# Sums of squares of a grouped norm: transposes and running sums in place of products with ones

## The reference

```python
N_GROUPS = 8
D_INNER = 2 * D_MODEL            # 2048, 256 channels a group
def ssd_branch(z, xbc, dt_raw, ...):
    xbc = silu(causal_depthwise_conv(xbc, conv_w, conv_b))
    ...
    y = ssd_chunked(...)                     # chunked scan of the 32 heads
    y = y * jax.nn.silu(z)
    yg = y.reshape(bsz, seqlen, N_GROUPS, D_INNER // N_GROUPS)
    yg = yg * lax.rsqrt(jnp.mean(yg * yg, axis=-1, keepdims=True) + RMS_EPS)
    y = (yg.reshape(bsz, seqlen, D_INNER) * norm_g)
    return y @ out_w
```

## Time and profile before

| | |
|---|---|
| time, median of 3 runs | 923.46 us (922.59 to 923.56) |
| profiled execution, first to last instruction | 922.0 us |
| TensorE matmuls busy | 910.9 us, 99% |
| VectorE busy | 752.3 us, 82% |
| ScalarE busy | 551.0 us, 60% |
| GpSimd busy | 18.3 us, 2% |
| granted TensorE clock, mean of the core | 0.999 |

### The profile page before, as it was taken

How to read it: one execution, slowest core, us unless ns; L and a number is a source line. 1 busy time by engine, 2 the same in 40 slices (tenths; PEclk the granted TensorE clock), 3 DMA queues, 4 the chain that set the end, 5 groups by cost and what they waited for, 6 DMA issues and landing times.

```text
span 922.0 us, 18238 instructions
## 1 busy us (share of the span) xinstructions
PE 910.9 (99%) x6625; PEld 860.2 (93%) x6625; DVE 752.3 (82%) x1373; ACT 551.0 (60%) x938; POOL 18.3 (2%) x30
## 2 busy tenths in 40 slices
PE   8999999999999999999999999999999999999997
PEld 6999989999999999998888888999999999999886
DVE  5999999999999888689888646798859988888543
ACT  5649666776667474556666535668455765666432
POOL 1000000000000000000000000100000000000000
PEclk9999999999999999999999999999999999999999
DMA  8576234545445537437555554455147455555601
GB/s 326 180 265 227 93 127 170 205 130 188 148 148 205 206 105 276 169 128 246 198 182 183 195 190 166 144 176 189 61 166 266 156 191 182 182 182 182 228 1 47
DMA packets 45470, 161.55 MB, mean 175 GB/s; under 512 B 5188, under 2 KB 5864, under 8 KB 45288
## 3 DMA queue, kind: packets, MB, share of 16 engines
q1 hardware_dynamic: 43488, 154.74, 48.6%
q10 hardware_dynamic: 1928, 6.08, 1.8%
HBM read 159.72 MB, written 1.09 MB: 174 GB/s over the span
## 4 chain that ended last, share of the span: by engine, by line
PE 62%; issue 24%; DVE 10%; ACT 1%; DMA 1%; POOL 0%; SPq 0%; DVEq 0%; POOLq 0%; ACTq 0%
PE A L436 8%; PE A L437 8%; PE A L438 8%; PE B L656 5%; PE A L465 4%; DVE w_lo L1330 3%; PE B L465 3%; PE B L436 2%; PE B L437 2%; PE B L438 2%; PE A L467 2%; DVE part L1366 2%; PE B L467 2%; PE B L737 2%; PE B L816 1%
## 5 line engine op out<-in xcount | busy, mean ns | idle before, releaser
L1330 DVE TENSOR_TENSOR w_lo<-raw,w_hi 128x1024 fp32r<-128x1024 f32 x265 | 321.5, 1220 | 67.7 <-ACT w_hi L888 66.2
L888 ACT ACTIVATE w_hi<-raw 128x1024 fp32r<-128x1024 f32 x265 | 276.4, 1052 | 79.6 <-PE A L738 20.9
L436 PE MATMUL A<-h,w_hi 128*128 128x256 f32 x952 | 274.1, 288 | 0.0
L438 PE MATMUL A<-h,w_lo 128*128 128x256 f32 x952 | 269.3, 283 | 0.0
L437 PE MATMUL A<-h,w_hi 128*128 128x256 f32 x952 | 269.3, 283 | 0.0
L436 PEld LDWEIGHTS A<-h,w_hi 128*128 128x128 f32 x952 | 182.2, 191 | 1.9 <-issue 1.8
L437 PEld LDWEIGHTS A<-h,w_hi 128*128 128x128 f32 x952 | 182.4, 192 | 0.2
L438 PEld LDWEIGHTS A<-h,w_lo 128*128 128x128 f32 x952 | 182.2, 191 | 0.0
L436 PE MATMUL B<-h,w_hi 128*128 128x256 f32 x352 | 100.9, 287 | 0.0
L437 PE MATMUL B<-h,w_hi 128*128 128x256 f32 x352 | 99.6, 283 | 0.0
L438 PE MATMUL B<-h,w_lo 128*128 128x256 f32 x352 | 99.6, 283 | 0.0
(11 more groups left out here) (301 smaller groups left out, 1560.8 us busy)
## 6 DMA issues: line engine op xcount, KB each, us to landing
raw<-in_weights_dram SPq DMA_DIRECT2D x289, 512.0 KB, 4.1
csrow<-cs_dram ACTq DMA_DIRECT2D x9, 512.0 KB, 4.5
x<-in_x_dram SPq DMA_DIRECT2D x4, 256.0 KB, 5.1
bd<-in_lru_w_dram ACTq DMA_DIRECT2D x1, 1024.0 KB, 6.8
out_dram<-m_wide SPq DMA_DIRECT2D x3, 256.0 KB, 2.1
raw<-in_weights_dram SPq DMA_DIRECT2D x2, 256.0 KB, 4.9
par<-in_params_dram SPq DMA_DIRECT2D x1, 379.0 KB, 7.1
out_dram<-m_wide ACTq DMA_DIRECT2D x2, 128.0 KB, 2.5
```

What stands on the lines that cost most here:

```text
L436: mm(dst, wh, lo, start=first, stop=False, skip_group_check=free)
L438: return mm(dst, wl, hi, start=False, stop=last, skip_group_check=free)
L888: F(w_hi[:, s, :], raw[:, s, :], ACT.Copy).then_inc(hi_ready, 1)
L1330: V.tensor_tensor(w_lo[:, s, :], raw[:, s, :], w_hi[:, s, :].bitcast(F32), ALU.subtract).then_inc(lo_ready, 1)
```

## The change

TensorE no longer multiplies squares with ones. As soon as the gated `y` is there it transposes `y`, four blocks of 128x128 into bank `A[3]`, so that tokens lie on the partitions and a group's 256 channels on the free axis. ScalarE squares each half (128 x 256) straight from PSUM and keeps a running sum over the free axis (`accum_out`) in a new tile `ysum` of 128 x 2. VectorE reads the moment from `ysum`.

In turns 1 to 7 the transposes stand in the middle of the second output piece. In turn 0, which has no output piece, they stand where the products with ones stood. On ScalarE the squares move: behind `first_taps` in the loop, and in the first turn from n = 6 to n = 8.

```diff
@@ in TensorE's program
-            def y_sums(g):
-                pe.wait_ge(ysq_ready, g + 1)
+            def y_transposes(g):
+                pe.wait_ge(yz_ready, g + 1)
                 for t in range(TT):
                     for c in range(2):
-                        ins = mm(sums[:, t:t + 1], ysq[:, c, t * P:(t + 1) * P], ones[:, 0:1],
-                                 start=c == 0, stop=c == 1)
-                ins.then_inc(sums_ready, 1)
+                        ins = nc.tensor.transpose(A[3][:, t * T + c * P:t * T + (c + 1) * P], y[:, c, t * P:(t + 1) * P],
+                                                  ident)
+                ins.then_inc(yt_ready, 1)
...
-            def out_piece(p, turn, g, c):
+            def out_piece(p, turn, g, c, between=None):
                 native_loaded(p, turn)
                 pe.wait_ge(scale_read, g + 2)
                 for m in range(KD):
+                    if between is not None and m == KD // 2:
+                        y_transposes(between)
                     ins = mm(acc_out(m), raw[:, p % RING, m * P:(m + 1) * P], yn[:, c, :], start=False, stop=False,
...
-            chain = {1: cb, 2: x_transposes, 3: y_products, 4: y_sums, 5: y_scale}
+            chain = {1: cb, 2: x_transposes, 3: y_products, 5: y_scale}
...
-                        out_piece(base + OUT_AT[s // 4], t, g - 1, s // 4)
+                        out_piece(base + OUT_AT[s // 4], t, g - 1, s // 4, g if s == 4 else None)
...
-            first_chain = {1: cb, 3: x_transposes, 5: y_products, 7: y_sums, 8: y_scale}
+            first_chain = {1: cb, 3: x_transposes, 5: y_products, 7: y_transposes, 8: y_scale}
@@ in ScalarE's program
             def y_squares(g):
-                act.wait_ge(yz_ready, g + 1)
-                F(ysq[:, :, :], y[:, :, :], ACT.Square).then_inc(ysq_ready, 1)
+                act.wait_ge(yt_ready, g + 1)
+                for t in range(TT):
+                    ins = F(ysq[:, t, :], A[3][:, t * T:(t + 1) * T], ACT.Square, accum_out=ysum[:, t:t + 1])
+                ins.then_inc(sums_ready, 1)
...
                 split(6)
+                act.wait_ge(cb_used, g + 1)
+                first_taps(g + 1, (0, 1))
+                act.wait_ge(yz_ready, g + 1)
+                first_taps(g + 1, (2, 3))
                 y_squares(g)
-                first_taps(g + 1)
                 drain_input(4, 4, base + IN_AT[4], t)
...
                     if n == 6:
+                        act.wait_ge(yz_ready, 1)
+                        first_taps(1)
+                    if n == 8:
                         y_squares(0)
-                        first_taps(1)
@@ in VectorE's program
             def y_mean(g):
-                moment_of(g + 2, 2 * P, RMS_EPS).then_inc(mean_ready, 1)
+                moment_of(g + 2, 2 * P, RMS_EPS, ysum[:, :]).then_inc(mean_ready, 1)
```

More of the change, by code:

```diff
@@ L223, in hybrid_kernel @@
         dt_parts = ysq[:, 0, :]
+        ysum = sb("ysum", [P, TT], scope=s3)
         s3.close()
@@ L331, in hybrid_kernel @@
         dec_ready, m_ready, y_ready, yz_ready = sem("dec_ready"), sem("m_ready"), sem("y_ready"), sem("yz_ready")
-        ysq_ready, first_tap = sem("ysq_ready"), sem("first_tap")
+        yt_ready, first_tap = sem("yt_ready"), sem("first_tap")
         conv_operand_ready, mixed_ready = sem("conv_operand_ready"), sem("mixed_ready")
@@ L681, in _ @@
                 if s in (1, 4):
-                    out_piece(GATES0 + OUT_AT[s // 4], 0, g - 1, s // 4)
+                    out_piece(GATES0 + OUT_AT[s // 4], 0, g - 1, s // 4, g if s == 4 else None)
                 if s in chain:
@@ L956, in ring, with first_taps @@
                 return A[o % 3][:, 0:T]
-            def first_taps(g):
+            def first_taps(g, js=range(4)):
                 act.wait_ge(drained, drained_by(g, 3))
                 dyn = not isinstance(g, int)
-                for j in range(4):
+                for j in js:
                     at = (g * 4 + j) * SSM_K + SSM_K - 1
```

## The result

The changed kernel takes 927.20 us (median of 5 runs, 925.48 to 927.62) against 923.20 us for the kernel before (5 runs, 922.59 to 923.56): ratio 1.0041, 95% interval 1.0030 to 1.0052. It is slower by 0.3 to 0.5%. 926.3 us had been forecast. The profiled execution has a span of 925.7 us against 922.0.

The account below looks back on a forecast made before the run. TensorE bounds turns 2 to 6, VectorE leads in turn 0, early turn 1 and late turn 7. Span 922.0 - 2.4 (loop) + 4.3 (stall) + 0.95 (clock) = 924.85, plus 1.46 gives 926.3 us; range 925.2 to 927.6, 80% 923.9 to 928.6.

Parts of the forecast that it names:

- The stall in turn 0: VectorE's moment waits 5.0 us for ScalarE's squares behind the exponents; 0.72 us absorbed, 4.3 us more.
- The clock: TensorE, idle 6.4 us in turn 0, restarts at 1.2 GHz; loses 1.6 us, 0.65 hidden, 0.95 us more.
- chance (a): Rival: turn 0's stall comes but TensorE's clock holds; 925.4 us, chance 0.20.
- The loop's gain: TensorE in turns 1 to 6: products with ones save 0.89 us, transposes cost 0.49; net 0.40 a turn, 2.4 us less.
- about 0.57 us of room: Loop: GpSimd's scale is ready at 166.12, TensorE takes it at 166.74; only gain above 0.57 us would be lost.
- one of the prediction's own signs of being wrong: Loop: the forecast is wrong if the scale starts to hold TensorE there.
- Where each turn's gain ends: Turns 1 to 6 pay 0.40 us each; in turns 0 and 7 the gain goes into TensorE's wait for the scale.
- That room on VectorE: VectorE's waits for TensorE in the loop, 0.98 us a turn, shrink to 0.58.
- The price of a transpose: TensorE: four cost 0.43 to 0.53 us, taken as 0.49; the page's 275 ns is a latency, not a cost.
- The sum: Whole kernel: 922.0 - 2.4 + 4.3 + 0.95 = 924.85 us for the span, 926.3 us for the median.
- The step from span to median: Whole kernel: the median stands 1.46 us above the profiled span, so 924.85 becomes 926.3 us.
- its three bounds: Whole kernel: stall 4.0 to 4.8 us, gain 1.8 to 3.3, clock 0 to 2.2.

Follow-up runs that it names:

- The run with early squares: Changed kernel with turn 0's squares on ScalarE moved ahead of the twelve exponents (n = 6 instead of n = 8): 921.95 us, ratio to the kernel before 0.9985.
- the one with the stall alone: Kernel before with turn 0's squares moved to n = 8 behind first taps, products with ones just ahead of the scale, no transposes: 930.71 us, ratio 1.0076.
- the run with fillers: Changed kernel plus 24 filler matmuls of 512 columns on TensorE while it stands idle in turn 0: 926.23 us, ratio to the kernel before 1.0033.
- the early moment: Changed kernel with turn 0's squares ahead of the exponents and, in turns 1 to 7, VectorE's moment ahead of the split: 920.29 us, ratio 0.9969.
- the fastest version: The same kernel as the early moment: squares of turn 0 ahead of the exponents, moment ahead of the split in turns 1 to 7: 920.29 us.

## Why the prediction was right

**The stall in turn 0** was the main term and came as forecast: ScalarE's squares at 111.14 (111.63 said, and the whole stage was 0.5 us earlier), VectorE's wait 4.95 us (5.0 said), the scale at 113.18 (113.7). Two squares with their sums took 0.72 us (0.8 said). The wait of 0.72 us for `w_hi` went. The run with early squares took the stall out and the one with the stall alone put it into the kernel before; both support the mechanism.

**The clock** fell, as forecast, with TensorE idle for 6.28 us (6.4 said), but this step's price was too small: 0.95 us. The slow stretch lasted until 118.9 and TensorE came to the scores of turn 1 19.25 us after the scale (113.18 to 132.43), where before 16.82 us had been enough (108.63 to 125.45, when it began to wait): 2.4 us lost where 1.6 was said. Of it, 0.6 us vanishes in the wait that TensorE has left when the clock holds, as the run with fillers shows (0.65 said), so 1.9 us net: twice the forecast. I had taken the first twelve fillers of the program as the measure; the input pieces kept the low level longer (5.8 us) and lose 0.094 us each. The weight loads behind every matmul, from which I had expected less to lose, slow down too: 0.33 us each at the low level, 0.19 at the high one. What reached the scores is 5.05 + 2.43 - 1.32 = 6.16 us, 0.9 over the forecast 5.25. In the run with fillers it is 4.25, so the stall had its 4.3 right and the clock carries the whole miss. All this is from one profiled execution of each; by the medians the clock carries about 1 us. The fall came some 5 us after the last matmul, where the end of the program had shown 2.7; it lay only 1.1 us ahead of the scale, so the forecast fall came with little to spare, and chance (a) was near.

**The loop's gain** had the right mechanism and a somewhat large size: 0.40 us a turn said, 0.33 measured. TensorE's own part was larger, 0.45, which the early moment brought out (28.28 to 27.83). The step that failed is "about 0.57 us of room" at the scale: I took it as a threshold for the whole gain. By the rows only 0.35 us was free (0.98 - 0.63 from GpSimd's end to the next matmul), and a path 0.45 shorter could win no more than that. So the scale did begin to hold TensorE in the loop, by 0.12 us a turn and without a wait in the list: one of the prediction's own signs of being wrong, and true in this small measure.

**Where each turn's gain ends** was right: turn 7 gained nothing, its wait for the scale went from 0.41 to 0.86 us. The output piece was not held by the wait for `y`, and VectorE's waits in the loop fell, at the scores from 0.5 to 0.15 us a turn; those before `xdt` stayed at 0.48. That room on VectorE did not become the bound.

**The price of a transpose** was right by the row (0.43 us for four, confirmed by doubling them). The row of a single one is 0.27 us long, which is a latency and not what it costs. The section of the Trainium skill on transposes ("TensorE: Matmul & The Clock Gate", "Part 4: PE-mode transpose") gives about 275 ns for one in a kernel, in bf16; the length of the f32 row here agrees with it, the cost of 0.11 us each doesn't.

**The sum.** 924.85 us had been said for the span, 925.7 came: 0.91 more at the scores of turn 1 (the clock), 0.44 less won between there and the end (the scale), and 0.49 because the stage began earlier in this execution, which is chance: 0.91 + 0.44 - 0.49 = 0.86. Both terms made the forecast too low, and the start of the stage covered over a third of that. The step from span to median held by luck: the time of each run lies 1.8 us above its own span, and the 1.46 came from a profiled execution slower than its median, as the one after the change is too (927.52 against 927.20). The stated range of 925.2 to 927.6 is narrower than its three bounds give if they fall together, 924.2 to 928.7.

## What to carry to other kernels

When an instruction moves within an in-order engine's program, price everything that it moves behind, in each copy of the loop: here the loop's six turns won 2 us and the one turn that is written out lost 6. A stall of some microseconds on a matmul engine can cost more than the wait that it adds: here 6.3 us without a matmul were followed by 5.8 us at the low level, while 1.3 us were not. Look at the granted clock in the windows behind the gap. A wait that is not listed can still be near: in this loop 0.16 us between the producer's end and the consumer's start already cost 0.12 us, and 0.32 cost nothing. When a producer comes that close to its consumer, move it ahead before counting a gain.

## What the hardware showed besides

The running sum of a ScalarE instruction appears as a second instruction of 0.20 us, with 0.09 us from start to start.

GpSimd's power function over 128x2 takes 0.86 us while VectorE does f32 taps (the row at 164.98 above), and 1.63 us when VectorE's 128x1024 split runs beside it; the kernel before has such a place too, 1.60 us at 331.07 with the split at 330.91. In the fastest version:

```profile
163.51 1.63 POOL L413 TENSOR_TENSOR scale<-moment,half 128x2 f32<-128x2 f32 x1 [25.98 <-DVE moment L1350]
```

The moment had moved ahead by 1.1 us, of which the scale kept only 0.4. That the split is the cause is read from which instruction overlaps in time, and was not tried by itself.

The time from TensorE's last matmul to the fall of the granted clock was not the same in three places: 2.7 us at the end of the kernel before, 2.4 us in turn 0 of the kernel with the stall alone (0.61 over the window from 109 to 111, last matmul over at 107.04), and about 5 us in turn 0 of the changed kernel (0.53 over the window from 112 to 114, last matmul over at 106.9).
